# Eight rings of weight tiles placed at other byte offsets in SBUF

## The reference

```
f, nq, nk, nv, cq, ckv, kr, g = split(h @ w_in)
y_f   = fourier_mix(f)
y_na  = neighbourhood_attention(nq, nk, nv, ...)
y_mla = latent attention of mla_queries(cq), mla_keys_values(ckv, kr)
out   = sum_b(sigmoid(g_b) * (y_b @ w_branch_b)) @ w_out
x     = layer_norm(ALPHA * x + (1 + g1) * out)
x     = layer_norm(ALPHA * x + (1 + g2) * ((silu(h @ w_gate) * (h @ w_up)) @ w_down))
```

## The kernel before

| ring | matmuls of 512, 256 columns | moving operand at | ring before at, distance |
|---|---|---|---|
| layer 0 projection | 480, 480 | 32 | 32, 0 |
| layer 0 gated and out, `ahi`/`alo` | 768, 768 | 32 | 32, 0 |
| layer 0 gated, `yhi`/`ylo` | 288, 288 | 32 | 32, 0 |
| layer 0 feed-forward | 1584, 1584 | 32 | 224, 192 |
| layer 1 projection | 480, 240 | 32 | 32, 0 |
| layer 1 gated and out, `ahi`/`alo` | 768, 0 | 32 | 32, 0 |
| layer 1 gated, `yhi`/`ylo` | 288, 0 | 32 | 32, 0 |
| layer 1 feed-forward | 1584, 0 | 32 | 224, 192 |
| second block projection | 384, 0 | 32 | 96, 64 |
| second block output | 192, 0 | 32 | 96, 64 |

## Time and profile before

### The profile page before, as it was taken

How to read it: one execution, slowest core, us unless ns; L and a number is a source line. 1 busy time by engine, 2 the same in 40 slices (tenths; PEclk the granted TensorE clock), 3 DMA queues, 4 the chain that set the end, 5 groups by cost and what they waited for, 6 DMA issues and landing times. The chain is left out here.

```text
span 3166.0 us, 37052 instructions
## 1 busy us (share of the span) xinstructions
PE 2905.9 (92%) x14705; PEld 2311.1 (73%) x14705; DVE 1687.5 (53%) x2379; ACT 1209.3 (38%) x1800; POOL 450.9 (14%) x445
## 2 busy tenths in 40 slices
PE   7998899999989999999799799998999978876995
PEld 4886566888868888887587457886888846555774
DVE  3385665233455656643315563446656454655997
ACT  5324555122243212222435443324323244635774
POOL 4400200000030000003400100002000124122332
PEclk9999999999989999999799899999999989887997
DMA  7860101222113444431720103334656335335962
GB/s 207 121 180 19 25 1 50 60 61 70 47 54 108 144 128 127 140 93 41 96 65 16 24 10 100 94 85 119 190 163 190 101 48 74 154 89 183 374 239 80
DMA packets 397871, 330.11 MB, mean 104 GB/s; under 512 B 38038, under 2 KB 340484, under 8 KB 397572
## 3 DMA queue, kind: packets, MB, share of 16 engines
q1 hardware_dynamic: 384196, 304.56, 34.1%
q0 software_dynamic: 13248, 23.13, 3.6%
q10 hardware_dynamic: 256, 0.07, 0.0%
HBM read 331.96 MB, written 30.33 MB: 114 GB/s over the span
## 5 line engine op out<-in xcount | busy, mean ns | idle before, releaser
L1184 PE MATMUL ps<-ahi,w_hi 128*128 128x512 f32 (+1 forms) x2264 | 767.8, 353 | 11.1 <-DVE w_lo L1211 11.1
L1185 PE MATMUL ps<-ahi,w_lo 128*128 128x512 f32 (+1 forms) x2264 | 766.8, 353 | 0.0
L1211 DVE TENSOR_TENSOR w_lo<-w_raw,w_hi 128x1024 fp32r<-128x1024 f32 (+2 forms) x242 | 339.8, 1406 | 373.9 <-ACT w_hi L1201 371.5
L1184 PEld LDWEIGHTS ps<-ahi,w_hi 128*128 128x128 f32 x2264 | 428.0, 189 | 76.7 <-DVE w_lo L1211 14.0
L1187 PE MATMUL ps<-alo,w_hi 128*128 128x512 f32 (+1 forms) x2264 | 473.5, 352 | 0.0
L1185 PEld LDWEIGHTS ps<-ahi,w_lo 128*128 128x128 f32 x2264 | 428.6, 189 | 60.0 <-issue 0.2
L1201 ACT CAST w_hi<-w_raw 128x1024 fp32r<-128x1024 f32 (+2 forms) x244 | 285.5, 1171 | 470.8 <-PE ps L1187 367.6
L1187 PEld LDWEIGHTS ps<-alo,w_hi 128*128 128x128 f32 x2264 | 376.6, 189 | 57.9
L937 DVE SCALAR_TENSOR_TENSOR vec_acc<-vec_w,csilu,vec_acc 128x512 f32<-128x512 f32 x364 | 257.2, 752 | 8.4 <-DVE vec_acc L937 5.7
L1351 POOL TENSOR_TENSOR xsum<-x 128x768 f32<-128x768 f32 (+1 forms) x4 | 6.4, 1592 | 1407.3 <-DVE x L1330 1407.3
L1274 DVE SCALAR_TENSOR_TENSOR x<-ps,mod,x 128x512 f32<-128x512 f32 x80 | 51.4, 668 | 233.7 <-PE ps L1187 220.7
(11 more groups left out here) (556 smaller groups left out, 5185.9 us busy)
## 6 DMA issues: line engine op xcount, KB each, us to landing
vec_w<-in_w_mod SPq DMA_DIRECT2D x128, 512.0 KB, 4.1
w_raw<-in_w_in SPq DMA_DIRECT2D x102, 512.0 KB, 4.3
e_raw<-in_w_gate SPq DMA_DIRECT2D x46, 512.0 KB
e_raw<-in_w_up SPq DMA_DIRECT2D x46, 512.0 KB
e_raw<-in_w_down SPq DMA_DIRECT2D x46, 512.0 KB
w_raw<-in_w_ffn_gate SPq DMA_DIRECT2D x44, 512.0 KB, 4.4
w_raw<-in_w_ffn_up SPq DMA_DIRECT2D x44, 512.0 KB, 4.0
w_raw<-in_w_ffn_down SPq DMA_DIRECT2D x32, 704.0 KB, 4.6
```

What stands on the lines that cost most here:

```text
L1184: pe.matmul(o, whi[:, j, b0 + b, :], hi[:, b, t0:t0 + tn], start=(b == 0), stop=False)
L1185: pe.matmul(o, wlo[:, j, b0 + b, :], hi[:, b, t0:t0 + tn], start=False, stop=False)
L1211: dve.tensor_tensor(wlo[:, j, 0:d.blocks, :], raw_of(d, i, jj), whi[:, j, 0:d.blocks, :].bitcast(F32), ALU.subtract).then_inc(lo_ready[j]. ...
```

## The change

A helper `place` pads the stack, with a tensor that nothing reads or writes, until the next tensor lies at a given address modulo 256. `new_ring` calls it before its three tensors, with 32 (where the moving operands lie) plus the ring's number from a list. No instruction is added, removed or moved on any engine; only addresses differ.

```diff
+        def place(ctx, at):
+
+            gap = (at - (nc.sbuf_base + 31) // 32 * 32) % 256
+            if gap:
+                names[0] += 1
+                ctx.enter_context(nc.sbuf_tensor(f"gap_{names[0]}", [P, gap // 4], F32))
+
...
+        RING_AT = iter([32, 96, 160, 224, 96, 160, 224, 32])
+
         def new_ring(c, blocks):
+            place(c, 32 + next(RING_AT))
             return (sb(c, "w_raw", [P, 2, blocks, P]), sb(c, "w_hi", [P, 2, blocks, P], F32R), sb(c, "w_lo", [P, 2, blocks, P], F32R))
```

## The result

The changed kernel takes 3190.69 us (median of 4 runs, 3185.81 to 3194.7), the kernel before 3161.07 us beside it (4 runs). The ratio is 1.009, with a 95% interval of [1.0074, 1.0106]: slower by 29.6 us, between 23 and 34 by the interval. The forecast was 3167.7. The profiled execution took 3194.7 us, its span is 3192.9 us against 3166.0, and the mean granted clock is 0.956 against 0.954. So the clock is not the cause.

The account below looks back on a forecast made before the run. Prediction: TensorE's matmul pitch bounds the ring stages. Interpolated terms of +9.5 us for 512 columns and -3.0 for 256 give +6.5 on 3161.22, so 3167.7 us; range of 8 in 10: 3140 to 3189.

Parts of the forecast that it names:

- I take the distance as the cause: Ring stages: distance between weights and moving operand sets the matmul pitch, since groups at equal distance agree across stages and layers.
- They lie on one line that falls by 1 ns for each 32 bytes: 512-column durations in ring stages: 396 ns at 64, 392 at 192, 390 at 256, interpolated for new distances.
- Distance 160: Both feed-forwards, moved from 192: 512 columns at 393 instead of 392 ns, 3168 matmuls, +3.2 us.
- the nearest row says 279: Layer 0's feed-forward, from 192 to 160: 1584 matmuls of 256 columns keep their duration, 0 us.
- 224: 512 columns at 391 ns: layer 1's projection +0.5 us, second block's projection -1.9 us.
- the middle: Distance 32, 512 columns at 393 ns, between 390 and 396: layer 0's projection +1.4 us, second block's output product -0.6.
- 96: Gated and out stages, 512 columns at 395 ns: +3.1 us in layer 0, +3.8 in layer 1.
- The 256 columns that leave distance 0: Projections and gated stages: 1488 matmuls at 281 instead of 283 ns, -3.0 us.
- clearly slower: Rival: weights at multiples of 64 bytes meet moving operands at 32 modulo 64 badly everywhere; +33.2 us, 3194.4 us, chance 0.15.
- The bounds -29 and +39: Limits in us on the whole change, with all rings at the shortest or longest back-to-back durations seen.
- The rival with the faster time: Odd multiples of 32 keep reads apart in every dense stage: 390 and 279 ns, -16.6 us, 3144.6 us, chance 0.29.
- several times shorter: Weight DMAs into the rings land much faster than the eight matmul pieces take, so their placement counts 0 us.

Follow-up runs that it names:

- e1: Changed kernel with all eight rings at distance 0 from their moving operand: 3157.22 us, ratio 1.0002 to the kernel before.
- e7: Changed kernel with `alo`, `a2lo`, all later tiles and all rings 32 bytes further on, `ahi` and `a2hi` staying: 3172.67 us, ratio 1.0039 to the kernel before.
- e2: Changed kernel with all eight rings at distance 128 instead: 3184.1 us, ratio 1.0081 to the kernel before.
- e3: Changed kernel with w_raw and w_hi at distance 0 and w_lo alone 32 bytes past: 3186.29 us, ratio 1.0083 to the kernel before.
- e10: Changed kernel with mapped ring distances 112, 192, 48 (layer 0), 208, 192, 208 (layer 1), 80, 144 (second block): 3172.37 us, one run.

## Why the prediction was wrong

The mechanism was right. TensorE's pitch bounds the ring stages, it depends on the distance, it passes to the end as far as the intervals tell (+31.7 us by the pitches, +29.6 measured), the products on `y` stay near theirs (1.6 ns less in layer 0, 0.9 more in layer 1), and no other engine matters. "I take the distance as the cause" was an inference from groups that agreed, and e1 and e7 show that it is so. That the two reads of SBUF get in each other's way is a further inference, which no run shows.

The step that failed is "They lie on one line that falls by 1 ns for each 32 bytes". Between 0, 64 and 192 there is no line. There is a plateau of about 233 ns (duration 396), with places below it: 0 and 240 above all, 176 and 192 less, 8 and 24 a little. As measured, six of the eight multiples of 32 lie on the plateau, and all four new distances are among them. By term:
- Distance 160, half of all matmuls: forecast 393, measured 395 and 396, as pitches 4.2 and 4.4 ns more than at 192 instead of 1. This is 13.6 us instead of 3.2. The 256 columns there went from 279 to 281 to 283, 5.5 us, where "the nearest row says 279" gave 0. Together 16 of the 25 us by which sum and pitches differ.
- 224 was put 1 ns above distance 0 and is 6 above it: 2.8 us instead of 0.5 in layer 1's projection, and 0 instead of -1.9 in the second block's.
- 32 was put at 393 as "the middle" and has 396: 2.5 instead of 1.4 us, and 0 instead of -0.6.
- 96 was nearly right, 396 and 397 for 395: 10.1 us instead of 6.9.
- The 256 columns that leave distance 0 were forecast at 281 and have 281, 280 and 279 (pitches 1.0, 2.0 and 2.5 ns shorter): 2.6 us of gain for 3.0.

The rival "clearly slower" had the places and nearly the price (+33.2, measured +29.6), and got 0.15. Its reason is refuted: e2 puts the weights at 32 modulo 64, like the moving operands, and is as slow. Its size held because 396 is the value nearly everywhere, and its 283 for 256 columns only at 160. The bounds -29 and +39 held the result, while the range of 3140 to 3189 ended 1.7 us short. That the bounds held was partly luck. They came from two lines of four-column weights, whose weights step by 16 bytes from block to block and so have no one distance, and whose medians went to 392 and 394 ns in the changed kernel although their own addresses stayed. The rival with the faster time is refuted for these four distances: it asked for a mean below 391, and they have 396. Its kernel of truth, that no known distance was best for both lengths, was followed up, and 240 comes near it.

One reading was wrong and cost nothing. The prediction has the weight DMAs land in a time "several times shorter" than the matmuls take. A load feeds one piece of 24 matmuls, about 5.6 us in the second block's projection, and takes 8.2 us there. TensorE did wait there for a split, 10.9 us before and 11.0 after, so the wait stayed and the count of 0 held.

What should have raised the chance of the slow case was already in the rows: 390, 392 and 396 at three distances, and one line of four-column weights at 397. Nothing showed an order in the distance. With three points and no known law, the next point is as likely at the worst of them as between them, and of the ring matmuls of 512 columns 45% started at the best distance and 46% at 192, 2 ns above it.

The rule of the Trainium skill ("TensorE: Matmul & The Clock Gate", Part 2: two independent read ports, so the next weight load does not steal from the running matmul) would have given 0. The traces disagree with a cost of 0 for these fp32r matmuls: the same instructions differ by 7 ns in 227, 3%, by addresses alone. The weight loads themselves kept their duration, 188 ns in layer 1's feed-forward at 192, 0 and 160 alike.

What stays open is the mechanism inside the chip, and whether a matmul's own weights count or those that load beside it. Nor do I know why layer 0's gated stage at 192 is at 232 ns and all others at 229, and by what a matmul's neighbours carry over (e3, e7, and the `y` products of e10 at 230.8 instead of 226.8 with distance 0 kept). The placement of w_raw was never varied by itself.

## What to carry to other kernels

Where back-to-back matmuls fill a stage and each has its own weights, the addresses of the moving operand and of the weights are a knob, worth about 1% in this kernel. It did best with both at the same value modulo 256 where the matmuls have 512 columns, and with the weights 192 bytes beyond where half of them have 256; 240 is the other place to measure. Other shapes and formats were not tried. Read the pitch over hundreds of back-to-back matmuls, not the mean duration, and never interpolate a property of addresses between a few points: one cheap run with another distance in each stage maps it.

## What the runs showed that I had not expected

- Four bytes are enough: at distance 4 the pitch of 512 columns is 232.4 ns against 226.6 to 229.4 at 0. At 240, 16 bytes on the other side, it is 227.0 to 228.7, and at 248 between them 233.3.
- 256 columns have another order: best at 192 (115.4 to 117.7 ns) and 8 (115.9), worst at 0, 112 and 160 (119.0 to 119.9). At distance 0 most pitches of 256 columns are one value, 120 ns, and of 512 columns 227; at other distances they spread more: the middle 80% go from 114 to 126 at 112 (256 columns) and from 228 to 237 at 4 (512 columns).
- The spread has an order. In layer 1's feed-forward the groups of eight on `alo` go round in three: 231.0, 231.6 and 237.4 ns at distance 160, 229.3, 231.5 and 226.1 at 192, and 226.8, 226.4, 226.8 at 0. So at 160 each matmul loses 4 to 5 ns and each third 11.
- Alternating distance 0 and 32 (e3) costs +28 us, as much as 128 throughout (e2, +26).
